# Attention scores from split queries and keys: three one-pass products in place of one four-byte product, two heads at a time

## The reference, cut to what matters

```python
# first stack: 4 query heads, 2 key heads, 64 wide, keys of the blocks n-1 .. n+1
scores = jnp.einsum("bnqhgd,bnkhd->bnhgqk", qb, kw) * (d ** -0.5)
scores = jnp.where(valid, scores, NEG_INF)
# first stack: 4 heads, 64 wide, keys of 8 rows of 64 positions, with a learned bias
scores = jnp.einsum("brqhd,brikhd->brhqik", qg, kg) * (d ** -0.5)
scores = jnp.where(col_ok, scores + bias, NEG_INF)
# second stack: 4 heads of two maps, 64 wide, all keys up to the query
s = jnp.einsum('bqhjd,bkhjd->bhjqk', qb, kb) * scale
s = s - slopes[None, :, None, None, None] * dist
a = p[:, :, 0] - lam * p[:, :, 1]          # p: softmax of s
```

## Time and profile before

| | |
|---|---|
| median of 3 runs | 3774.08 us (3770.61 to 3774.63) |
| span of the profiled execution | 3768.5 us |
| PE busy | 3636.0 us, 96% of the span |
| PEld (weight loads) busy | 2873.4 us, 76% |
| DVE busy | 1829.1 us, 49% |
| ACT busy | 704.6 us, 19% |
| POOL busy | 1308.4 us, 35% |

### The profile page before, as it was taken

How to read it: one execution, slowest core, us unless ns; L and a number is a source line. 1 busy time by engine, 2 the same in 40 slices (tenths; PEclk the granted TensorE clock), 3 DMA queues, 4 the chain that set the end, 5 groups by cost and what they waited for, 6 DMA issues and landing times.

```text
span 3768.5 us, 44735 instructions
## 1 busy us (share of the span) xinstructions
PE 3636.0 (96%) x16872; PEld 2873.4 (76%) x16872; DVE 1829.1 (49%) x2567; ACT 704.6 (19%) x1417; POOL 1308.4 (35%) x549
## 2 busy tenths in 40 slices
PE   8999999999998999999999999999998999999997
PEld 6777667777766788667888888888875788888886
DVE  5667536568536424576432422451447654143146
ACT  2220232120134000363100100110025411000002
POOL 3324203323303333203443444553220244444443
PEclk9999999999999999999999999999999999999998
DMA  3101202111201111101111111111110011111112
GB/s 130 40 29 40 53 12 62 51 29 34 64 12 34 34 51 34 56 1 40 45 50 50 45 50 50 50 57 50 37 59 7 29 45 47 48 50 50 45 50 73
DMA packets 60995, 168.98 MB, mean 45 GB/s; under 512 B 20640, under 2 KB 21024, under 8 KB 60832
## 3 DMA queue, kind: packets, MB, share of 16 engines
q1 hardware_dynamic: 39168, 142.62, 12.1%
q10 hardware_dynamic: 21664, 24.19, 2.2%
HBM read 159.45 MB, written 4.19 MB: 43 GB/s over the span
## 4 chain that ended last, share of the span: by engine, by line
PE 65%; DVE 3%; issue 2%; ACT 1%; DVEq 0%; ACTq 0%
PE ps L455 57%; PE ps L516 3%; PE ps L562 2%; PE ps L545 1%; DVE in_lo L1094 0%; DVE space_hi L1192 0%; PE ps L482 0%; PE ps L725 0%; ACT st L862 0%; DVE st L1103 0%; PE ps L721 0%; PE ps L573 0%; DVE st L1129 0%; PE ps L493 0%; PE ps L707 0%
## 5 line engine op out<-in xcount | busy, mean ns | idle before, releaser
L398 POOL TENSOR_TENSOR w_hi<-w_raw,ones 128x1024 fp32r<-128x1024 f32 x272 | 531.2, 1953 | 2398.5 <-PE ps L455 2394.4
L455 PE MATMUL ps<-in_hi,w_hi 128*128 128x512 f32 x3584 | 1138.2, 399 | 54.0 <-DVE in_lo L1094 21.7
L455 PE MATMUL ps<-in_hi,w_lo 128*128 128x512 f32 x3584 | 1116.3, 393 | 0.0
L455 PE MATMUL ps<-in_lo,w_hi 128*128 128x512 f32 x3584 | 1115.0, 392 | 0.0
L455 PEld LDWEIGHTS ps<-in_hi,w_hi 128*128 128x128 f32 x3584 | 661.2, 189 | 214.5 <-DVE in_lo L1094 26.7
L455 PEld LDWEIGHTS ps<-in_hi,w_lo 128*128 128x128 f32 x3584 | 671.9, 189 | 152.9 <-issue 13.4
L455 PEld LDWEIGHTS ps<-in_lo,w_hi 128*128 128x128 f32 x3584 | 674.4, 189 | 146.4 <-issue 4.4
L402 POOL TENSOR_TENSOR w_lo<-w_raw,w_hi 128x1024 fp32r<-128x1024 f32 x272 | 776.8, 2856 | 21.3
L1079 DVE TENSOR_TENSOR st<-ps,rfac 128x1024 f32<-128x1024 f32 x148 | 181.1, 1224 | 757.8 <-PE ps L455 726.5
L1085 DVE TENSOR_TENSOR xt<-xt,ps 128x1024 f32<-128x1024 f32 x112 | 136.7, 1221 | 413.3 <-PE ps L455 411.0
L516 PE MATMUL ps<-st 64*128 64x384 f32 (+3 forms) x704 | 250.0, 535 | 9.2 <-DVE small L1192 9.1
(11 more groups left out here) (147 smaller groups left out, 2598.4 us busy)
## 6 DMA issues: line engine op xcount, KB each, us to landing
w_raw<-w_in SPq DMA_DIRECT2D x272, 512.0 KB, 3.5
xt<-x_in ACTq DMA_DIRECT2D x8, 512.0 KB, 8.9
space_lo<-c_alibi ACTq DMA_DIRECT2D x2, 2048.0 KB, 8.0
out<-xt ACTq DMA_DIRECT2D x8, 512.0 KB, 3.0
st<-st ACTq DMA_DIRECT2D x24, 128.0 KB, 2.7
st<-c_rope ACTq DMA_DIRECT2D x2, 1024.0 KB
space_lo<-rpb_in ACTq DMA_DIRECT2D x2, 960.0 KB, 7.3
space_lo<-rpb_in ACTq DMA_DIRECT2D x2, 944.0 KB, 12.3
```

The source lines that it names most:

```text
L398: pool.tensor_tensor(w_hi[:, j, :], w_raw[:, j, :], ones[:, 0:1].broadcast_to([P, KC * P]), ALU.mult).then_inc(pool_own, 1)
L455: last = pe.matmul(ps[:, 2 * j + h, :], w[:, w_slot, (w_k + k) * P:(w_k + k + 1) * P], part[:, k0 + k, h * HALF:(h + 1) * HALF], start=(k ...
```

## The change

A float32 score product is replaced by three float32r products, high query by high key, low query by high key, high query by low key, added up in PSUM. ACT copies a chunk of keys or a round's queries to float32r (`key_hi`, `query_hi`); DVE subtracts that from the source (`key_lo`, `query_lo`; the keys' low part takes the source's place). The queries' parts have room for two rounds, and are made two rounds ahead. Bank 4 holds the head on the partitions 0 to 63 and bank 5 the one on 64 to 127, for gqa and na as well: these now compute two heads (t even and t+1) at a time, one piece in each step. The three products of one head are issued, then the three of the other. PE waits until both banks are read.

```diff
                 def scores(u, i):
                     n, t = units[u]
+                    if t == 0 and i == 0:
+                        pe.wait_ge(qk_lo.handle, qk_lo.at(stack, l, split_index(kind, n)))
+                    _, q_hi, q_lo = query_parts(kind, n)
+                    c = t if kind == "dif" else t // 2
+                    _, k_hi, k_lo = key_parts(kind, c)
                     for piece in pieces_of(tiles_of_round(kind, n))[i:i + 1]:
-                        for j in range(maps):
-                            q, base = query(t, j)
-                            p = state["p"]
-                            if p >= 2:
-                                pe.wait_ge(biased.handle, biased.at(stack, l, p0 + p - 1))
-                            pe.matmul(ps[:, 4 + p % 2, 0:len(piece) * P],
-                                      q[base:base + HD, n * P:(n + 1) * P],
-                                      key(t, j)[base:base + HD, piece[0] * P:(piece[-1] + 1) * P],
-                                      start=True, stop=True).then_inc(scored.handle, 1)
-                            state["p"] += 1
+                        p = state["p"]
+                        if p >= 2:
+                            pe.wait_ge(biased.handle, biased.at(stack, l, p0 + p))
+                        cols = slice(piece[0] * P, (piece[-1] + 1) * P)
+                        for j in range(2):
+                            for q, k in ((q_hi, k_hi), (q_lo, k_hi), (q_hi, k_lo)):
+                                rows = slice(HD * j, HD * (j + 1))
+                                last = pe.matmul(ps[:, 4 + j, 0:len(piece) * P], q[rows, c, :], k[rows, cols],
+                                                 start=(q is q_hi and k is k_hi), stop=(k is k_lo))
+                                if k is k_lo:
+                                    last.then_inc(scored.handle, 1)
+                        state["p"] += 2
...
                 def step(u):
                     if 3 <= u < len(units) + 3:
                         turn(u - 3, 0)
-                    if u < len(units):
+                    if u < len(units) and kind == "dif":
                         scores(u, 0)
...
                     if u < len(units):
-                        scores(u, 1)
+                        if kind == "dif":
+                            scores(u, 1)
+                        else:
+                            scores(u - u % 2, u % 2)
...
+            def query_hi(stack, l, kind, n, p0=0):
+                if n >= 2:
+                    act.wait_ge(scored.handle, scored.at(stack, l, p0 + pieces_before(kind, n - 1)))
+                source, hi, _ = query_parts(kind, n)
+                act.activation(hi, source, ACT.Copy).then_inc(qk_hi.handle, 1)
...
+                    if kind != "dif" and 3 <= u < len(units) + 3:
+                        groups(u - 3, 1)
                     if 1 <= u < len(units) + 1:
                         exps(u - 1)
-                    if 3 <= u < len(units) + 3:
+                    if kind == "dif" and 3 <= u < len(units) + 3:
                         groups(u - 3, 1)
+                    if u % 4 == 1 and 2 <= u // 4 + 1 < NB:
+                        query_hi(stack, l, kind, u // 4 + 1, p0)
...
+            def key_lo(stack, l, kind, c, index):
+                source, hi, lo = key_parts(kind, c)
+                dve.wait_ge(qk_hi.handle, qk_hi.at(stack, l, index))
+                dve.tensor_tensor(lo, source, hi.bitcast(F32), ALU.subtract).then_inc(qk_lo.handle, 1)
...
+                key_lo(1, l, "dif", 0, 1)
+                key_lo(1, l, "dif", 1, 2)
                 evacuate(1, l, 22, st[:, 14, :])
+                key_lo(1, l, "dif", 2, 3)
                 evacuate(1, l, 23, st[:, 15, :])
...
+                query_lo(1, l, "dif", 0)
+                query_lo(1, l, "dif", 1)
+                key_lo(1, l, "dif", 3, 4 + 2)
```

More of the change, by code:

```diff
@@ L127, in products_done, with pieces_before @@
     return i + 1 if i < first else min(first + 2 * (i - first + 1), first + KC + i - first + 1)
+def pieces_before(kind, n):
+    lanes = 2 if kind == "dif" else 1
+    return sum(4 * lanes * len(pieces_of(tiles_of_round(kind, m))) for m in range(n))
 STEPS = 4 * NB + 8
@@ L196, in build @@
         xt = sb("xt", [P, KC, S])
+        base_xt = top[0] - 4 * KC * S
         base_in = top[0]
@@ L1027, in _ @@
                     last.then_inc(r_squared.handle, 1)
+                act.wait_ge(taken.handle, taken.at(1, l, 19))
+                for c in range(3):
+                    key_hi(1, l, "dif", c)
                 for c in (0, 1, 2):
@@ L1173, in scores @@
                     for piece in pieces_of(tiles)[i:i + 1]:
-                        for j in range(maps):
-                            m = maps * u + j
-                            i = maps * t + j
-                            first = cur[:, C_SINK + t:C_SINK + t + 1] if kind == "gqa" else 3.0e38
+                        for j in range(2):
+                            m = 2 * u + j if kind == "dif" else u + j
+                            i = 2 * t + j if kind == "dif" else t + j
+                            first = cur[:, C_SINK + i:C_SINK + i + 1] if kind == "gqa" else 3.0e38
                             dve.wait_ge(scored.handle, scored.at(stack, l, p0 + state["p"] + 1))
@@ L1254, in step @@
                             finish(n).then_inc(mixed_out.handle, 1)
+                    if u < len(units) and kind != "dif":
+                        scores(u - u % 2, u % 2)
                     if kind == "dif" and u % 4 == 1 and u >= 9:
                         rsqrt(stat[:, 0:4], root[:, 0:4], tmp[:, 0:4], (2,))
-                    if u < len(units):
+                    if u < len(units) and kind == "dif":
                         scores(u, 1)
+                    if u % 4 == 2 and 2 <= u // 4 + 1 < NB:
+                        query_lo(stack, l, kind, u // 4 + 1)
                     for n in range(NB):
@@ L1395, in _ @@
                 gate_input(1)
+                key_lo(0, l, "gqa", 0, 1)
+                query_lo(0, l, "gqa", 0)
+                query_lo(0, l, "gqa", 1)
                 steps = attention(0, l, "gqa", 0, 0, 0,
```

101 lines of the change are left out of this document (79 added, 22 removed).

## The result

The changed kernel takes 3747.75 us (median, 3745.82 to 3753.63), the kernel before took 3773.41 us beside it: ratio 0.9938, 95% interval 0.9924 to 0.9951. The forecast was 3684 us, in a range of 3662 to 3750. The sign was right and the gain, 26 us, was under a third of the 90 forecast. 3746 is what the second rival gave, but the trace refutes that rival's mechanism: its total was met by other causes.

What follows compares the result with a forecast made beforehand. PE, busy 96% of the span, was taken as the bound. Per layer gqa 19, na 26 and dif 0 us, 90 over both layers, off the 3768.5 span plus 5.6 to the median: 3684 us, range 3662 to 3750.

Steps and rivals of the forecast that it cites:

- the second rival: All scores: products start in program order, five passes a pair, 1.28 us at 512 columns; 14 us gained per layer, 3746; chance 0.15.
- the way in: Turning loads ahead of scores in gqa and na: 0.32 us saved for each score group fewer, 5.1 and 7.7 us a layer.
- its own signs of being wrong: A pair taking more than three passes, dif growing by over 5 us, or the stretch behind gqa growing.
- The pair: Two heads' scores side by side, three passes deep: 0.51, 0.675 and 0.84 us for 256, 384 and 512 columns.
- The lower bound, nothing: Least gain allowed for the way in, if the new place behind the values costs as much again.
- na's exponentials: na, rounds 2 to 5: second piece scored late, a new wait of 0.5 to 0.65 us in 8 steps; 5 us lost.
- the 1 us for DVE: na: splitting, bias and `add_to_x` push DVE's first reading by up to 1.2 us; 1 us lost.
- The start of dif: `query_lo` twice behind `add_to_x` gives PE its queries at 1559.5, not 1556.8: 2.8 us lost, bounds 0 and 4.
- dif's banks: dif: PE needs both banks read, 0.7 us later; 0.35 us in each of 12 steps, 4 us lost, bounds 0 and 8.
- dif's shorter scores: Score line in dif: 40.4 us before, 33.1 after, a gain of 7 us a layer.
- gqa's gain reaches the end: Stretch behind gqa, where DVE is the bound: it begins and ends 19 us sooner, PE's wait staying 5.8 us.
- The forecast's own lower edge: Low end of the forecast's own range: 3665 us, with no loss to banks, 2.8 us or late exponentials.

Runs made afterwards that it cites:

- the four mends: Changed kernel with a wait for each bank in dif, dif's splits early, ACT's `query_hi` behind `split_hi`, gqa's scores between turning and turning back: ratio 0.9836 to the kernel before.
- the 8 taps: Kernel with the four mends, plus 8 convolution taps from between the evacuations of blocks 18 and 19 computed in gqa's steps: 3685.94 us, ratio 0.9777.
- the 10 taps: Kernel with the four mends, plus 10 of DVE's convolution taps computed one block earlier, one more in each of gqa's ten blocks: ratio 0.9858.

## Why the prediction was wrong

Its views led to the right price of a score and to wrong prices for what lies round it. A layer of each kind was to give 45 us: 19 in gqa, 26 in na, nothing in dif with its start. It gave 13 and 15, and dif with its start lost 16. The step that failed in the first stack is the way in, counted as a gain where the scores' move cost time; in dif it is the start, priced as if DVE worked alone, and the 7 us for shorter scores. One of its own signs of being wrong showed: dif grew by over 5 us.

- **The pair: right.** Three passes deep, the heads side by side, 0.56, 0.73 and 0.90 us for the 0.51, 0.675 and 0.84 forecast. The earlier trace rows were read rightly.
- **The way in: the term that failed first.** It was to give 5.1 us a layer in gqa and 7.7 in na. The row, 0.65 us for three turning loads, held two things. 0.12 of the 0.32 is what every load behind a block's 512-column matmul takes (0.23 and not 0.11), and stays; only 0.20 was the score's. And the way in remains in the new place (0.26 us behind the values, and in 15 steps of na still 0.31 behind a turning, where 0.11 is usual). The lower bound, nothing, was not low enough either: PE's time on turnings and values grew by 1.5 us a layer in gqa and 6.4 in na, since the score had covered ACT's copy out of bank 6 and, in na, DVE's reading of bank 7. (The Trainium skill, "TensorEngine Tiling (Array Packing)", Key Properties, has TensorE drain at each change of the tiling mode; both entries, 0.20 and 0.15 us over the usual, agree.) Against the forecast that is 6.6 and 14.1 us a layer, 41 us in all. The prediction does not ask what ACT did while the moved score ran, though the earlier trace rows show it: the values wait for ACT's copy behind the score.
- **na's exponentials: 5 us a layer that did not occur.** The turnings wait for no exponential; they would, and na would take 15.5 us more, in the old order of ACT, a line of the change that the forecast did not price. This and the 1 us for DVE offset a part of the error above.
- **The start of dif: mis-sized.** Forecast 2.8 us. Measured 5.3 of wait on average of the two layers, 2.4 more for the block's own input (ACT's two `query_hi` of 0.6 stood ahead of its `split_hi`; with their order turned round, in the four mends, the 2.4 went), and the half clock after the wait. Moving DVE's three splits gave back 18 us in all. The prices came from instructions that ran alone or, as `add_to_x`, with one input in PSUM. POOL's splitting stood at that very place in the kernel before, beside the second of the earlier trace rows, though the rows do not show it:

```profile
1556.93 1.90 POOL L398 TENSOR_TENSOR w_hi<-w_raw,ones 128x1024 fp32r<-128x1024 f32 x1 [12.81 <-PE ps L455]
```

- **dif's banks: right.** 4 us a layer forecast (0 to 8); 3.9 and 7.9 by the trace with the waits given up, 4.9 and 2.5 with the wait added to the kernel before, where the time shows it too.
- **dif's shorter scores: no gain.** 7 us were forecast, from 40.4 on the score line. That sum leaves out what PE waits for the second bank inside the pairs; the line took 51.4 us. It did fall in the first layer, by 12.5 us, but PE's time on the turnings ahead of them, where the wait now shows, rose by 13.3. A pair that waits for DVE's reading is not shortened by a shorter product. How much of this is the half clock is not shown apart: with DVE's splits early, the start and dif got back 8.4 and 10.8 us a layer, and the wait was only some 5 of these.
- **gqa's gain reaches the end: right, as far as it went.** The wait behind gqa was 5.4 us for 5.8. It was not slack without end: the next 4 us sank into it.
- **The second rival** came out right in its sum of 14 us a layer by chance. Its premise, 1.28 us a pair at 512 columns, is refuted by 0.90.
- **The forecast's own lower edge** is off by 5 us: without the losses named (4, 2.8 and 5 us a layer) the sum gives 3660, not 3665.

Left open: why na's first layer got 17.1 us of half clock in the four-mend kernel (some 7 us longer, though nothing was edited there), while the second did not. With the 8 taps it is there again, with the 10 taps not. The profiled execution of the 8 taps, 3693.59 us, is 6 to 8 us longer than its four others, at a clock of 0.985 for 0.988 and 0.989, so the half clock may come in some executions only.

## What to carry to other kernels

Before an instruction is moved, list what the other engines do while it runs in its old place: the stall that it hides comes back when it leaves. With the way in, the difference was 41 us here, nearly half of the forecast gain. Price an added instruction by its slowest row beside the neighbours that it will have, and look for the engine's idle stretch just ahead of the place. And test the parts apart: computing two heads at a time gave over four fifths of the gain in the first stack, without the split that came with it and brought the losses.

## What the runs showed that was not expected

- Products of two halves of the partitions run side by side whatever their order in the queue: 0.90 us at 512 columns both ways.
- DVE's subtraction of 128x512 with both inputs in SBUF (the on-chip memory of the tiles) takes 0.69 us, and up to 2.82 when POOL's splitting runs at the same time, ending 0.55 us behind POOL both times. DVE's `add_to_x`, which reads PSUM, takes its 1.22 us beside POOL's instruction as well (1504.69 above).
- Within 5.7 us of idle PE the granted clock falls to its half, 1.2 GHz, and it stays there for 10 of the 14 us behind them (0.63), so that a pair of 128 columns holds PE 0.84 us; without the wait it holds 0.49.
- A total of waits is no price. Waiting for both banks doubled the waits ahead of dif's scores (12.4 to 24.9 us in the first layer) and cost 4.9 us.
